# Thirty-two indirect gathers of expert rows: into buffers with DVE's adds, or adding into X themselves

## The reference

```python
for l in range(DEPTH):
    ...
    x = x + g1[:, None, :] * y                      # the mixer
    h = modulate(rms_norm(x, norm_ffn_g[l]), sh2, sc2)
    x = x + g2[:, None, :] * grouped_moe(h, ...)    # two experts per token
return rms_norm(x, final_norm_g)
```

## Time and profile before

| | us |
|---|---|
| median of three runs | 1817.98 |
| span of the profiled execution | 1812.5 |
| TensorE busy | 1533.8 (85%) |
| DVE busy | 856.0 (47%) |
| ACT busy | 258.0 (14%) |
| POOL busy | 150.2 (8%) |

### The profile page before, as it was taken

How to read it: one execution, slowest core, us unless ns; L and a number is a source line. 1 busy time by engine, 2 the same in 40 slices (tenths; PEclk the granted TensorE clock), 3 DMA queues, 4 the chain that set the end, 5 groups by cost and what they waited for, 6 DMA issues and landing times.

```text
span 1812.5 us, 17004 instructions
## 1 busy us (share of the span) xinstructions
PE 1533.8 (85%) x5355; PEld 850.0 (47%) x5356; DVE 856.0 (47%) x1548; ACT 258.0 (14%) x507; POOL 150.2 (8%) x267
## 2 busy tenths in 40 slices
PE   3799999989955999999359989987997489999980
PEld 2684544458843444444134334432886344444430
DVE  3554686644243332232353999966224422223326
ACT  2210000001121111111130000005112011111112
POOL 2000000000000111011310000000001011011104
PEclk9999999999986999999769989998999599999995
DMA  9574066560143666794532335442004567556727
GB/s 334 160 279 154 25 217 210 169 202 1 47 181 121 231 221 219 268 327 155 189 128 65 99 91 131 105 107 81 1 1 163 186 221 281 200 189 238 281 80 280
DMA packets 196430, 300.79 MB, mean 166 GB/s; under 512 B 12021, under 2 KB 153425, under 8 KB 196384
## 3 DMA queue, kind: packets, MB, share of 16 engines
q1 hardware_dynamic: 169952, 205.94, 36.1%
q0 software_dynamic: 17696, 62.24, 9.5%
q10 hardware_dynamic: 8736, 31.99, 4.5%
HBM read 248.51 MB, written 51.53 MB: 166 GB/s over the span
## 4 chain that ended last, share of the span: by engine, by line
PE 63%; DMA 16%; DVE 13%; issue 2%; ACT 2%; SPq 1%; POOL 1%; DVEq 0%; POOLq 0%; ACTq 0%
PE bank L886 19%; PE bank L964 15%; PE bank L1005 13%; DMA W<-in_moe_w_down 12%; PE bank L1020 6%; DVE W L1183 3%; DVE R L1604 3%; PE bank L996 2%; DVE R L1161 2%; PE bank L1109 1%; DMA W<-in_ada_w 1%; PE bank L869 1%; DVE X L1161 1%; PE bank L1142 1%; PE bank L903 1%
## 5 line engine op out<-in xcount | busy, mean ns | idle before, releaser
L886 PE MATMUL bank<-HTR,W 128*128 128x512 f32 x1024 | 451.4, 599 | 7.2 <-DVE R L1591 7.2
L1005 PE MATMUL bank<-W,R 128*128 (+1 forms) x816 | 369.5, 606 | 31.0 <-DMA W<-in_moe_w_down 14.2
L886 PEld LDWEIGHTS bank<-HTR,W 128*128 128x128 f32 x1024 | 193.9, 192 | 244.6 <-issue 244.0
L1161 DVE TENSOR_TENSOR R<-bank,R 128x256 f32<-128x256 f32 (+1 forms) x91 | 49.3, 542 | 540.6 <-ACT R L686 339.0
L1005 PEld LDWEIGHTS bank<-W,R 128*128 128x128 f32 x816 | 153.0, 192 | 217.8 <-issue 213.8
L964 PE MATMUL bank<-W,R 128*128 128x256 f32 x1024 | 231.1, 385 | 9.0 <-ACT R L786 7.8
L964 PEld LDWEIGHTS bank<-W,R 128*128 128x128 f32 x1024 | 194.6, 193 | 38.6 <-ACT R L786 8.7
L1604 DVE SCALAR_TENSOR_TENSOR R<-R,PT 128x998 f32<-128x998 f32 (+21 forms) x152 | 195.1, 1284 | 5.4
L1020 PE MATMUL bank<-W,R 128*128 x408 | 187.1, 602 | 3.8 <-DVE R L1412 3.8
L1183 DVE SCALAR_TENSOR_TENSOR W<-W,CAB 128x256 f32<-128x256 f32 x308 | 149.3, 485 | 11.0
L1020 PEld LDWEIGHTS bank<-W,R 128*128 128x128 f32 x408 | 74.7, 193 | 79.7 <-issue 79.7
(11 more groups left out here) (191 smaller groups left out, 945.6 us busy)
## 6 DMA issues: line engine op xcount, KB each, us to landing
W<-in_ada_w SPq DMA_DIRECT2D x48, 1024.0 KB, 11.6
W<-in_moe_w_gate SPq DMA_DIRECT2D x32, 1024.0 KB, 7.4
W<-in_moe_w_up SPq DMA_DIRECT2D x32, 1024.0 KB, 11.0
W<-in_moe_w_down SPq DMA_DIRECT2D x32, 1024.0 KB, 12.9
y_scratch<-R ACTq DMA_DIRECT2D x51, 512.0 KB, 7.5
W<-glu_scratch SPq DMA_DIRECT2D x48, 258.0 KB, 4.6
W<-in_conf_w SPq DMA_DIRECT2D x12, 1024.0 KB, 8.8
W<-in_hyb_w_in SPq DMA_DIRECT2D x10, 1024.0 KB, 12.9
```

Source lines behind the costliest of these rows:

```text
L886: ins = pe.matmul(dst[:], lhs(k), rhs(k), start=(k == 0), stop=(k == kc - 1))
L1005: ins = pe.matmul(M[0][:], XT[:, k, :], W[:, bass.ds(at + k * 2 * FE, 2 * FE)], start=(k == 0), stop=(k == KC - 1))
L1161: return dve.tensor_tensor(o, a, b, op)
```

## The change

The buffers Y1 and Y2, DVE's `combine` and the semaphore `xup` are gone. Each gather names the block of X as its destination and addition as its operation, so that the DMA adds the row it fetches to what is there. The order within each half is written out: the four gathers of s = 0, then the four of s = 1, each of the latter after a wait for the first gather of the same block. ACT's squares wait for `c_in[l][b][1]` instead of `xup`. DVE has the scalings of the norm alone.

```diff
--- before.py
+++ after.py
@@ -242,13 +242,6 @@
         def hv(n):
             return HTR[:, n, :]
 
-        Y1, Y2 = ([HTR[:, 3 * n + b, :] for b in range(3)] + [R[:, 3 - n, b * D:(b + 1) * D] for b in range(4)]
-                  for n in range(2))
-        NY0, NY = 3, 7
-
-        def y_of(b):
-
-            return b if b < NY else NY0
         GBF = hv(6)
         FGB = hv(7)
         OUTS = [XN[b // 4][:, b % 4, :] for b in range(NB)]
@@ -300,7 +293,6 @@
         v_ok = sem("v_normed")
         ya_ok = sem("head_a_output_ready")
         gb_in = [sem(f"gate_rows_in{n}") for n in range(4)]
-        xup = sem("x_updated")
         dch = sem("dve_step")
         act_ch = sem("act_step")
         conv_ok = sem("conv_ready")
@@ -600,14 +592,13 @@
                 pool.wait_ge(xg_in[l], nt * 16 + 16)
                 pool.wait_ge(held[l], nt + 1)
                 pool.tensor_tensor(PSCR[:, l:l + 1], PSCR[:, 2:3], PSCR[:, 2:3], ALU.add).then_inc(held[l], 1)
-                for b in range(NB):
-                    if b == NY:
-                        pool.wait_ge(xup, 8 * l + NY0 + 1)
-                    for s, dst in ((0, Y1), (1, Y2)):
-                        pool.indirect_dma_start(
-                            out=dst[y_of(b)], out_offset=None, in_=y_dram,
-                            in_offset=bass.IndirectOffsetOnAxis(ap=SLOTU[:, s, b:b + 1], axis=0)
-                        ).then_inc(c_in[l][b][s], 16)
+                for b, s in [(b + 4 * h, s) for h in range(NH) for s in range(TOPK) for b in range(4)]:
+                    if s:
+                        pool.wait_ge(c_in[l][b][0], 16)
+                    pool.indirect_dma_start(
+                        out=X[:, b, :], out_offset=None, in_=y_dram,
+                        in_offset=bass.IndirectOffsetOnAxis(ap=SLOTU[:, s, b:b + 1], axis=0),
+                        compute_op=ALU.add).then_inc(c_in[l][b][s], 16)
                 if l == 0:
                     pool.wait_ge(tapc_in, 16 * SH * SH)
                     pool.wait_ge(quads_ok, 1)
@@ -647,7 +638,7 @@
                     act.wait_ge(xl[h], 16)
                 for b in range(4 * h, 4 * h + 4):
                     if r:
-                        act.wait_ge(xup, 8 * (r // 2 - 1) + b + 1)
+                        act.wait_ge(c_in[r // 2 - 1][b][1], 16)
                     link(act.activation(JUNK, X[:, b, :], ACT.Square, accum_out=SS[:, b:b + 1]))
                 s = slice(4 * h, 4 * h + 4)
                 act.activation(SD[:, s], SS[:, s], ACT.Sqrt, bias=EPSC[:], scale=1.0 / D).then_inc(rms_sd, 1)
@@ -1427,15 +1418,6 @@
                     tile_out(t - 1)
                     turned(t)
                 tile_out(nt - 1)
-
-            def combine(l, b):
-
-                for s, y in ((0, Y1), (1, Y2)):
-                    dve.wait_ge(c_in[l][b][s], 16)
-                    ins = tt(X[:, b, :], X[:, b, :], y[y_of(b)], ALU.add)
-                    if s == 0:
-                        link(ins)
-                ins.then_inc(xup, 1)
 
             def router_weights(l):
 
@@ -1577,10 +1559,7 @@
             route(0)
             experts(0)
 
-            for b in range(NB):
-                if b == 5:
-                    rms_apply(2, 0)
-                combine(0, b)
+            rms_apply(2, 0)
             evict_ht(2, 1, 0, 0)
             rms_apply(2, 1)
             evict_ht(2, 1, 0, 1)
@@ -1627,10 +1606,7 @@
 
             route(1)
             experts(1)
-            for b in range(NB):
-                if b == 5:
-                    rms_apply(4, 0)
-                combine(1, b)
+            rms_apply(4, 0)
             rms_apply(4, 1)
```

## The result

The changed kernel takes 1847.5 us, the median of four runs (1843.69 to 1855.99), against 1819.4 us for the kernel before on the same chip. The ratio is 1.0167, 95% interval 1.0138 to 1.0197: 30 us slower, 25 to 36. The profiled execution has a span of 1841.9 us, 29.4 us over that of before. It took 1843.69 us, so what lies around the span is 1.8 us; the 5.5 us that the prediction put there came mostly from the spread between runs.

A forecast was written before the change was run, and what follows sets the result against it. The serial stretch from the gathers to the last square bounds each layer's end, with POOL, DMA and DVE near balance. Dearer gathers add 15.5 us in layer 0 and 19.5 in layer 1: 1818 + 35 = 1853 us, range 1843 to 1872.

The forecast's parts named there:

- The price of a gather: DMA time of one adding gather of 128 rows: two passes, 1.53 + 1.29 = 2.82 us.
- 32 p - 55.3: Change in us over both layers' gather stretches, p being one gather's price; zero at p = 1.73 us.
- the fixed part of a landing: Part of the first gather's 4.4 us from issue to landing that does not depend on its price: 2.87 us.
- the first pass: DMA engines fetching a gather's rows from DRAM, priced at the plain gather's 1.53 us.
- The low end that I named: Lower price for an adding gather on the DMA engines: two reads both at the output store's rate, 2.59 us.
- POOL's waits: Eight waits per layer on POOL for a block's first gather before its second is issued; taken as zero.
- Its longer issue: POOL making descriptors for the second read: up to 2.2 us a gather with the gap, covered by DMA's 2.82 us.
- SP's later load: Layer 0's load of two more weight tiles waits for the last gather and moves with it; zero.
- The stores between the gathers: Layer 1's four stores of half 0 fall among half 1's gathers and share the engines: 5.2 us.
- A: Rival on the DMA engines: addition nearly free, a gather stays at 1.53 us; 1807 to 1812 us, chance 0.18.
- B: Rival on the DMA engines: reads overlap in part, 1.7 to 2.5 us a gather; 1817 to 1843 us, chance 0.10.
- C: Rival on the DMA engines: separate trips or smaller pieces, 3.4 us or more a gather; 1894 us at 4.1, chance 0.14.

The follow-up runs named there:

- e1_plain: The changed kernel with every gather overwriting its block of X instead of adding; 1803.8 us, ratio 0.9934 to the kernel before.
- e2_no_adds: The kernel before with DVE adding only 8 of the 1024 columns of each block; 1807.6 us, ratio 0.9950 to the kernel before.
- e3_all_first: The changed kernel with the first gathers of all eight blocks issued before all second ones; 1847.1 us, ratio 1.0164 to the kernel before.
- e5_stores_last: The changed kernel with SP waiting for layer 1's last gather before storing output blocks; 1843.9 us, ratio 1.0146 to the kernel before.
- pe8_sums: The kernel before with TensorE summing both buffers of every block in PSUM, DVE adding the sum to X; 1828.9 us, ratio 1.0063.

## Why the prediction was right

**The bound and the sign.** The stretch was read rightly as serial behind the last block of X, and POOL, DMA and DVE as near balance. Taking DVE out and charging DMA made DMA the bound (e1_plain: the addition alone accounts for 16 to 17 us a layer). The last squares, forecast near 48 and 53 us, came at 44.2 and 49.4.

**The price of a gather, the term that was mis-sized.** I took 2.82 us; it is 2.52. The sum 32 p - 55.3 gives 25.3 us with the measured price, against 27.4 us in the stretches. Most of the rest is the fixed part of a landing: 2.87 us in the sum, 6.2 - 2.52 = 3.7 us measured, of which 0.6 us is the longer issue. That the addition costs a second pass was right; the first pass, 1.53 us, was too dear. It rested on reading the busy share of 93 to 95% as a limit, "there is no idle share for a second stream to hide in". The gathers of the kernel before were fed too slowly: without DVE's adds a plain gather costs 1.28 us (e2_no_adds). Twice that is 2.56, near the 2.52 measured. The low end that I named, two reads both at the store's rate, 2.59 us, was the right row. The Trainium skill's rule of "Collectives: The Full Stack" ("The bandwidth ceiling: the fold count and why AG ≠ RS ≠ AR"), two reads per chunk and a factor of 1.93, measured there between two collectives, agrees: 2.52 / 1.28 is 1.97. It had to be applied to a gather that is kept fed, not to the 1.53 us in the trace. Whether it is the read or the arithmetic that fills the time no run here separates.

Nor was 1.53 us the pace at which the gathers of the kernel before landed. SP's load that waits for the last gather of layer 0 starts 29.2 us after the first issue (918.71 less 889.49), where the formula had 27.4:

```profile
918.71 1.01 SPq L473 DMA_DIRECT2D W<-in_conf_w  x2
```

So DVE was 3.3 us behind the gathers there (32.5 less 29.2), not 5.1. In e2_no_adds the same load starts at 25.0 us: of the 7.2 us that the adds cost layer 0, 4.2 went through the slowed gathers and 3.0 through DVE's lag.

**What was costed at nothing.** POOL's waits: zero by e3_all_first, though they add up to 16.6 us. Its longer issue, 1.84 us a gather with the gap where I allowed 2.2: covered by 2.52. SP's later load: the first product follows the last square by 18.7 us, 19.0 before. The stores between the gathers: 5.2 us predicted, 5.2 measured (49.4 less 44.2), gone from the stretch in e5_stores_last. A slip that changed no term: three other gathers, not four, lie between the two of a block.

**The rivals.** A needed p under 1.73 us. It did not come, yet what spoke for it was real: bursts of 420 GB/s and POOL's slow issue beside adds meant that DVE's adds cost the kernel before 13.0 us in both stretches (e2_no_adds), where I had 11.4 for its lag behind the gathers. B, reads that overlap in part, ends at 2.5 us, so that the measured price lies on its edge with the forecast's case. C is excluded by the price and by the first landing, 6.2 us. (The chances do not quite add up: "faster" is given 0.19, but A, which is all of it, has 0.18.)

The forecast was +35 us and the measured change +28 to +30. Two errors stand in it with opposite signs: a gather was priced 0.3 us too high (32 x 0.3 = 9.6 us), nearly all of it in the first pass, and the longer fixed part was left out (1.7 us). That the time fell inside the forecast's own range of 1843 to 1872 us is in part luck, as the measured price stands at that range's lower edge.

## What to carry to other kernels

Before a DMA is made to add, price its gather at the rate it has when nothing holds back its issue, and double it (here 2 x 1.28 us, 2.52 measured); the adds on a compute engine must cost the path more than that second pass to pay for it, and here DVE's 1.23 us a gather was not even on the path in full. A DMA busy share near 1 does not say that the queue is at its limit: look at the GB/s beside it, and at whether the issues come as closely as they can. Where an engine sits idle beside the one that ends last, as ACT did, try moving an instruction between them first: here that brought the last square of layer 0 forward by 4.1 us, where the change put it back by 11.7.

## What the runs showed of the hardware that I had not expected

- DVE's adds with both inputs in SBUF stretch POOL's issue of an indirect gather from 0.94 up to 1.98 us, 1.22 us on average in layer 0. With one input in PSUM (pe8_sums) it stays at 0.94, and with 8 columns per add (e2_no_adds) too, but for two issues beside DVE's scaling of half 0 (1.13 and 1.88 us). The Trainium skill, "SBUF — State Buffer", "Who interferes with whom", says that such a DVE instruction contends with GpSimd's reads; it also infers that descriptor generation, which writes, is not held up by it. The first agrees with these runs. The second does not carry over to an indirect gather, which also reads its row numbers from SLOTU in SBUF; whether it is this read or the making of descriptors that is held up, no run here separates.
- An adding gather's issue takes 1.53 us on POOL against 0.94 for a plain one, with nothing beside it: in e3_all_first, where no work of DVE falls beside the issues, all 32 take 1531 to 1592 ns. Beside DVE's scaling of half 0 the changed kernel's take up to 1.97 us.
- The accumulation leaves no trace in the counts of packets and bytes: 196430 and 300.79 MB in the kernel before and in the changed one.
